# Second block's attention: key transposes inside the value projection, two weight chunks behind the first maxima, half-output steps reordered

## The reference, cut to what matters

```
h = rms_norm(x, pre_norm_g[l]);  proj = h @ w_in[l]
aq, ak, av, ag, bq, bk, bv, bg = split(proj)
# differential attention: 4 heads, two score maps each, with a relative-position bias
sc = einsum(q, k) + bias;  p = softmax(sc);  a = p[0] - lam * p[1];  oa = a @ v
ya = rms_norm(oa, diff_subln_g[l]) * (1 - lam_init) * silu(ag)
# grouped attention: 8 query heads on 2 key heads, rotary positions
yb = softmax(q @ k.T) @ v * silu(bg)
x = x + rms_norm(concat(ya, yb) @ w_out[l], post_norm_g[l])
```

## Time and profile before

| | us |
|---|---|
| three runs | 1072.59, 1074.46, 1081.99 |
| median | 1074.46 |
| profiled execution, its own time | 1074.91 |
| span of the profiled execution | 1073.2 |
| PE busy | 1033.4 |
| DVE busy | 765.9 |
| ACT busy | 549.8 |

### The profile page before, as it was taken

One profiled execution on the slowest core, in us unless ns is written; L12 is line 12 of the kernel. 1 busy time (PEld: TensorE's weight loads), 2 busy tenths in 40 slices (PEclk: granted clock), 3 DMA queues, 4 the chain that ended last, 5 costly groups with the idle time before them and its releaser, 6 DMA issues.

```text
span 1073.2 us, 17088 instructions
## 1 busy us (share of the span) xinstructions
PE 1033.4 (96%) x6050; PEld 903.5 (84%) x6050; DVE 765.9 (71%) x1368; ACT 549.8 (51%) x918; POOL 101.6 (9%) x160
## 2 busy tenths in 40 slices
PE   6999999999999999999999999999999999899997
PEld 5888787899999988889999899999988788787775
DVE  5688878997888677776877765544678675686663
ACT  1357755544544456644444454434464665565662
POOL 0031201000000010110100000000012020220200
PEclk9999989999999999999999999999999999999999
DMA  9776756588787648857676356664446620366300
GB/s 369 287 260 216 250 182 216 196 306 297 266 273 272 231 155 308 300 199 254 208 247 226 120 190 195 207 203 157 158 149 212 217 84 16 126 213 207 120 11 40
DMA packets 57197, 218.46 MB, mean 204 GB/s; under 512 B 6420, under 2 KB 11540, under 8 KB 51000
## 3 DMA queue, kind: packets, MB, share of 16 engines
q1 hardware_dynamic: 48368, 169.24, 46.3%
q0 software_dynamic: 6048, 43.52, 11.3%
q10 hardware_dynamic: 2728, 5.00, 1.5%
HBM read 216.67 MB, written 1.06 MB: 203 GB/s over the span
## 4 chain that ended last, share of the span: by engine, by line
PE 83%; DVE 8%; ACT 4%; DMA 3%; issue 1%; POOL 1%; SPq 0%; DVEq 0%; ACTq 0%; POOLq 0%
PE ps L1740 24%; PE ps L1741 24%; PE ps L1742 24%; DVE w_lo L1007 2%; PE ps L1844 2%; PE ps L1809 1%; PE ps L2226 1%; DMA ada_raw<-in_adastream 1%; PE ps L1799 1%; ACT w_hi L554 1%; PE ps L1789 1%; PE ps L2112 1%; PE ps L2274 1%; ACT both L914 1%; DMA arena<-in_adastream 1%
## 5 line engine op out<-in xcount | busy, mean ns | idle before, releaser
L1007 DVE TENSOR_TENSOR w_lo<-raw,w_hi 128x1024 fp32r<-128x1024 f32 (+1 forms) x312 | 355.7, 1181 | 68.8 <-ACT w_hi L554 63.9
L554 ACT ACTIVATE w_hi<-raw 128x1024 fp32r<-128x1024 f32 (+1 forms) x312 | 306.5, 1021 | 137.7 <-DMA raw<-in_wstream 99.7
L1740 PE MATMUL ps<-h_hi,w_hi 128*128 128x256 f32 x704 | 200.8, 285 | 1.4 <-DVE h_lo L1086 1.0
L1742 PE MATMUL ps<-h_hi,w_lo 128*128 128x256 f32 x704 | 199.2, 283 | 0.0
L1741 PE MATMUL ps<-h_lo,w_hi 128*128 128x256 f32 x704 | 199.2, 283 | 0.0
L1740 PE MATMUL ps<-w_hi,h_hi 128*128 128x512 f32 (+1 forms) x480 | 191.4, 399 | 6.3 <-DVE h_lo L1086 3.1
L1741 PE MATMUL ps<-w_lo,h_hi 128*128 128x512 f32 (+1 forms) x480 | 185.6, 387 | 0.0
L1742 PE MATMUL ps<-w_hi,h_lo 128*128 128x512 f32 (+1 forms) x480 | 185.6, 387 | 0.0
L1740 PEld LDWEIGHTS ps<-h_hi,w_hi 128*128 128x128 f32 x704 | 134.9, 192 | 4.7 <-issue 2.4
L1740 PE MATMUL ps<-w_hi,a_hi 128*128 128x512 f32 x352 | 137.3, 390 | 0.6 <-DVE a_lo L1460 0.6
L1741 PE MATMUL ps<-w_lo,a_hi 128*128 128x512 f32 x352 | 137.2, 390 | 0.0
(11 more groups left out here) (221 smaller groups left out, 1343.8 us busy)
## 6 DMA issues: line engine op xcount, KB each, us to landing
raw<-in_wstream SPq DMA_DIRECT2D x296, 512.0 KB, 5.3
ada_raw<-in_adastream POOLq DMA_DIRECT2D x40, 1024.0 KB, 5.8
ada_raw<-in_adastream SPq DMA_DIRECT2D x4, 1024.0 KB, 9.2
arena<-in_adastream SPq DMA_DIRECT2D x4, 1024.0 KB, 10.8
row<-in_gate_rows ACTq DMA_DIRECT2D x5, 512.0 KB, 4.0
raw<-in_wsmall SPq DMA_DIRECT2D x16, 128.0 KB, 2.2
row<-in_params POOLq DMA_DIRECT2D x2, 769.0 KB, 5.4
x<-in_x SPq DMA_DIRECT2D x1, 1024.0 KB, 9.5
```

What stands on the lines that cost most here:

```text
L554: act.activation(w_hi[:, c % SPLIT, at], raw[:, n, 0:width // 2], ACT.Copy)\
L1007: nc.vector.tensor_tensor(w_lo[:, c % SPLIT, at], raw[:, (2 * c + h) % RAW, 0:width // 2], w_hi[:, c % SPLIT, at].bitcast(F32), ALU.subtract)\
L1740: nc.tensor.matmul(dst, sh, mh, start=start, stop=False)
L1742: return nc.tensor.matmul(dst, sl, mh, start=False, stop=stop)
```

## The change

The same arithmetic is done by the same instructions; only their places in the streams differ, in both layers.

- PE: the value projection (chunks 10 and 11) is written as four quarters, and the key transposes 5 and 6 stand between its second and third quarter. Before they stood behind it.
- ACT and DVE: units 5 and 6 are copied and split before chunk 13. Chunks 14 and 15 are no longer split ahead of the first maxima: on ACT chunk 14 lies between the two evictions of the values and chunk 15 behind `exps(1)`; on DVE half 0 of chunk 14 lies ahead of `maxima(0)`, half 1 ahead of `difference(0)`, and chunk 15 behind it.
- DVE: `difference(3)` goes ahead of `llo(18, 0)`; `first_output(3)` and `first_gated(2)` go ahead of `llo(18, 1)`; `first_gated(3)` goes ahead of `second_output(8)`; and `llo(19, 0)` goes behind `maxima(11)`.

```diff
@@ ACT
                 lsplit(12, CW)
-                lsplit(13, CW)
-                evict(4, av, (0, 1))
                 for u, k in ((5, 0), (6, 2)):
                     transposed(u, tiles_of(qk2_hi[:, 1, k:k + 2]), 1.0)
+                lsplit(13, CW)
+                evict(4, av, (0, 1), (0,))
                 lsplit(14, CW)
-                lsplit(15, CW)
+                evict(4, av, (0, 1), (1,))
...
                 exps(1)
+                lsplit(15, CW)
                 probs_copy(0)
@@ DVE
                 lsplit(12)
-                lsplit(13)
                 for u, k in ((5, 0), (6, 2)):
                     second_lo(u, tiles_of(qk2_lo[:, 1, k:k + 2]), tiles_of(qk2_hi[:, 1, k:k + 2]),
                               1.0)
-                lsplit(14)
-                lsplit(15)
+                lsplit(13)
...
+                llo(14, 0)
                 maxima(0)
                 maxima(1)
+                llo(14, 1)
                 difference(0)
+                llo(15, 0)
+                llo(15, 1)
                 maxima(2)
...
                 first_gated(1)
+                difference(3)
                 llo(18, 0)
-                difference(3)
                 first_output(2)
                 operand_lo(0, 2, layer * 4 + (4 + 1))
                 gate_product(b_gate, (0, 1), 2)
                 maxima(8)
                 maxima(9)
+                first_output(3)
+                first_gated(2)
                 llo(18, 1)
-                first_gated(2)
-                first_output(3)
-                llo(19, 0)
+                first_gated(3)
                 second_output(8)
-                first_gated(3)
                 maxima(10)
                 maxima(11)
+                llo(19, 0)
                 second_output(9)
@@ PE
-                lproject(10, (0, 1), 20)
-                pe.wait_ge(s_cp, layer * 12 + 6)
-                transposed(5, tiles(ak, 0, 1))
-                transposed(6, tiles(ak, 2, 3))
...
+                gate_step(10, (0, 1), 0, 0)
+                gate_step(10, (0, 1), 0, 1)
+                pe.wait_ge(s_cp, layer * 12 + 6)
+                transposed(5, tiles(ak, 0, 1))
+                transposed(6, tiles(ak, 2, 3))
+                gate_step(10, (0, 1), 1, 0)
+                gate_step(10, (0, 1), 1, 1)
                 score_pair(0)
```

More of the change, by code:

```diff
@@ L871, in gate_tanh, with evict @@
                                        scale=rpre_half[:, t:t + 1]).then_inc(s_gtanh, 1)
-                def evict(j, dst, banks):
-                    for t in range(TT):
+                def evict(j, dst, banks, tokens=range(TT)):
+                    for t in tokens:
                         ready(j, t)
```

## The result

| | before | after |
|---|---|---|
| median of 14 runs each, us | 1073.55 | 1062.79 |
| lowest and highest | 1069.19, 1081.99 | 1058.99, 1068.07 |
| ratio, 95% interval | | 0.9891, 0.9869 to 0.9913 |
| profiled execution, its own time | 1074.91 | 1061.2 |

The kernel is faster by 1.09%, with an interval of 0.87 to 1.31%. On the median of 1074.46 that the prediction was made against, the ratio is a gain of 11.7 us, with an interval of 9.3 to 14.1. The forecast was 9.6, just inside that interval.

What follows compares the result with a forecast made beforehand. PE, busy 1033.4 of 1073.2 us, bounds the kernel; only its idle or low-clock time can go. Gains of 9.9 and 2 x (0.75 - 0.1) make 11.2, less one 1.6 us clock fall 9.6: 1064.8 us, range 1062 to 1069.

Steps and rivals of the forecast that it cites:

- border: Whole kernel: a measurement can tell about 1% from no change, 10.7 us, so faster means below 1063.7 us.
- Part 1: Key transposes moved inside the value projection: PE's 1.71 us idle before the first scores goes, 1.75 us gained a layer.
- Part 2: Weight splits moved behind the first maxima: no wait before the first probability transposes, 2.45 us gained in layer one, 3.95 in two.
- The gain is 2.45: First layer, score_pair(0) to values(0): 13.32 us becomes 10.87 with weight splits behind the first maxima.
- Queues that are passed: Weight loads: chunk 15 is loaded 4 us later yet lands before ACT asks for it, with under 1 us of slack.
- "slower" rival: Chunk 15's later load holds up ACT before the first probability copies and everything behind waits: 1078 us, chance 0.04.
- Part 3: difference(3) ahead of a weight split of chunk 18: PE's transposes start earlier, 0.75 us gained a layer.
- part 4: Half output steps moved up: the 1.0 us wait goes, but llo(19, 0) delays the next operand; -0.1 us a layer.
- The clock: Half output: about 2.0 us of idle time close together makes the clock fall in one of two layers, costing 1.6 us.
- the rival that took nothing off: No fall of the clock behind the half output's gathered gaps, so the whole 11.2 us comes: 1063.2 us, chance 0.30.

Runs made afterwards that it cites:

- Part 2 alone: Chunk 14's second half and chunk 15 split behind the first maxima, key transposes in their old place; against the kernel before: 1065.81 us, ratio 0.9922.
- part 1 alone: Key transposes inside the value projection, chunks 14 and 15 still split ahead of the first maxima; against the kernel before: 1076.79 us, ratio 1.0029.
- parts 3 and 4 alone: Only difference(3) ahead of chunk 18 and the half output's steps reordered, old order before them; against the kernel before: 1075.75 us, ratio 0.9992.

## Why the prediction came out as it did

The time lay inside the range. The side was wrong: the larger chance, 0.61, went to a change below 1%, at 9.6 us against a border of 10.7, where 11.7 came. The measured interval, 9.3 to 14.1 us, holds both the forecast and the border, so the times alone do not show which term was off; the stretches do. Each of them came out as reckoned against the first profile, while one entry of the sum, what the clock costs the old front, was too small.

- **Part 1** was forecast at 1.75 us a layer. From the transposes of units 3 and 4 (833.51 before, 830.91 after) to the first scores it was 15.41 us and is 13.64, a gain of 1.77. It holds, but only with part 2: alone it gave nothing, since DVE's chain, with the late loads in it, took the place of the gap. The prediction gave it a price of its own, as if it stood by itself.
- **Part 2** is the step that failed, in the term for the first layer: "The gain is 2.45". Read off the two profiles that number was right (4.28 us from the transposes to `values(0)` with part 1, against 4.2). As a number for the kernel it was not. The prediction itself said that both layers lose the same time in two forms, and then charged the second layer 3.95 and the first 2.45, as one execution happened to have them. Over the six score stretches the old front costs 18.99 - 14.97 = 4.0 us a layer, with part 1 some 11.5 in both layers instead of 9.9. Of the 4.0, 2.5 is DVE's chain (17.47 - 14.97), and 1.5 is the mean cost of the falls. Part 2 alone gave 8.4, that is 4.2 a layer, though the interval of that run (5.6 to 11.1) also holds the prediction's 6.4.
- **Queues that are passed.** The load of chunk 15 was named the thinnest point, and it was: ACT waited 0.23 us for it. The experiment with part 1 alone shows the mechanism of the "slower" rival when nothing covers it.
- **Part 3 and part 4**, 0.65 us a layer: measured 0.63, with the gated product's gap gone and the next wait grown from 0.56 to 1.40. That `llo(19, 0)` gives it back is shown by moving that one line, 0.87 us a layer.
- **The clock.** One fall at 1.6 us was taken off. The size was right for most falls (1.4 to 1.6), and so was the rate of one layer in two (3 of 6 layers; 1 of 4 in the changed kernel itself). In the changed kernel's first profile neither layer fell; there the idle time was read in these windows:

```profile
887.00:891.00 4.00, 2.60 (x18) 2.10 (x17) 2.98 (x9) 2.37 (x7) 0.00 (x0) 1.00 0.13 37
```

  What was wrong is that the fall was set against the new kernel alone. The old kernel's falls behind its 1.71 and 2.31 us gaps were taken from one execution, where one of them lay hidden. The rows above at 0.50 behind a gap of 1.40 us show that the new kernel has falls too, so the rival that took nothing off (1063.2) was near the time for another reason than its own. The Trainium skill, TensorE: Matmul & The Clock Gate, section "HAM oscillation — how this bites in real kernels", has the clock fall only over gaps longer than the 1.40 to 2.53 us behind which it fell here; by these rows that doesn't hold for this kernel.

With that entry set right the sum is 11.5 + 2 x 0.63 - 1.5 (half a fall in each layer) = 11.3 us, against 11.7 measured. Both counts of the clock are small. Without the kernel of parts 3 and 4 alone, whose profile was of its slowest execution, the old stretch is 18.62 on the mean and the sum 10.6; with one fall in four layers instead of three in six it is 12.0. The gain is that of the front. By this reckoning the reordered half output earns 1.3 us and pays 0.8 to 1.5 back in falls of the clock, which fits that the change without it runs as fast; no run separates two times 1 us apart.

## What to carry to other kernels

A stretch whose low clock lies in a different place in each of two layers can be worth the same in both: take a loss from several executions or at least from all repetitions of the stage, and count falls of the clock on both sides of the comparison. When small idle times are moved together in front of one instruction, look which step now stands last on the engine that feeds it; here one weight split moved behind the wanted operand was worth 0.87 us a layer, more than the whole reordering of the half output (0.63). Whoever moves a split of streamed weights also moves the load that it frees: follow the slot to the half that will land in it. Without cover, ACT's waits of 0.78 and 2.05 us for two such halves helped to lose all that part 1 gains.

## What the runs showed of the hardware

- The granted clock falls behind short gaps, and not every time. Behind gaps of 0.41 and 1.40 us, with 0.66 us of transposes between them, it fell in 3 of 6 layers; behind 1.71 us in 1 of the 8 layers of the four profiles that have it; behind 2.29 to 2.32 us in 5 of 5; behind 2.53 us in both layers. Mostly it was back within four microseconds, but in three layers it stayed at 0.50 for six, seven and ten. Two executions of one kernel differ in this. How much of the spread of the times it makes was not measured: the first profile of the kernel before lost 1.6 us less in the score stretches than the second, and yet its execution was 1.5 us longer (1074.91 against 1073.39). What decides it in a given execution stays open.
- One of the executions of the kernel with `llo(19, 0)` moved took 2014.29 us, where all others of it lie between 1055.24 and 1067.59. Its repetition has none like it, up to 1061.41. The cause is not known.
